# Opening a fused two-block transformer kernel in quarters of the features

## The chip, the cores and the metric

The kernel runs on 1 core of one Trainium2 chip. The metric is the device time of one execution in microseconds; lower is better. The kernel before took 1553.04 us (median of 3 runs, 1551.54 to 1555.72).

## The reference, cut to what matters

The program computes two transformer blocks over 256 tokens of 1024 features, all in float32: a first one (HGRN2 branch, windowed attention branch, 32-expert mixture) and a second one (stick-breaking attention, convolution, 32 smaller experts). The change is in the first few operations of the first block:

```python
cond = jax.nn.silu(c)                                   # (1, 1024)
mod = cond @ w_ada[l] + b_ada[l]                        # (1, 6144): sh1, sc1, g1, sh2, sc2, g2
h = rms_norm(x, norm1_gain[l]) * (1.0 + sc1) + sh1      # (256, 1024)
proj = h @ w_in[l]                                      # 1024 x 4864, in ten column blocks
hq, hf, hi, hg, aq, ak, av, gate_h, gate_a = split(proj)
```

Feature k of h needs only its own entries of sc1 and sh1, that is one column each of w_ada; but the sum over k in h @ w_in needs all 1024 features, in any order.

## The kernel before, in words

Every engine has its own instruction list, written out by hand in one order; semaphores join them. There is no planner.

Large weights arrive by DMAs of 2 MB that SyncE (SP) issues from one list, `PRE` (line 95), each into one of the numbered slots. An entry waits until the unit that was in its slot has been used (`unit_free`). All small things come otherwise: rows of c, lower bounds, convolution weights and gains, part of the constants, positions and b_ada by ten DMAs that ScalarE issues (lines 1175 to 1184), and nine gains, sinks and biases plus six pieces of router weights by DMAs that GpSimd issues (lines 1119 to 1133), the first nine counted by the semaphore `smalls`.

`ada(n)` (line 1514) multiplies one 2 MB unit of w_ada by the conditioning vector. Units ada 0 to 3 hold, for all of sc1 and sh1, two of the eight groups of 128 input features each; so no entry of the modulation is complete before all four units have been summed. Then VectorE adds b_ada (line 1984), TensorE transposes the row into columns (line 1542), and VectorE forms shift and scale columns (lines 1988, 1989).

`x` is normalised by VectorE (line 1958), transposed by TensorE (`transpose_h`), and modulated twice: ScalarE writes the upper part `hT_up` in the fast float32r type (line 1207), VectorE writes it in full (line 1996) and subtracts (line 2003), which gives `hT_low`.

The projection runs in rounds; round r is column block r of w_in. In each, a weight piece is split in the same way: `split_upper` (ScalarE, line 359) and `split_lower` (VectorE, line 364), 2048 columns each; the lower half of piece 0 alone is made by GpSimd (line 1114). TensorE then sums three products: upper by upper, lower by upper, upper by lower. Round 0 (aq, 512 columns, `first_tokens`) is two pieces of four feature groups each; round 1 (ak and av, 256 columns) is one piece; round 2 (hf) and round 3 (hq) are two pieces each, cut by columns, 96 products of 256 columns. TensorE's order is round 0, ada 4, round 1, round 2, ada 5, ada 6, round 3, then the transposes of q and k (line 1563).

After round 1 VectorE copies keys and values, waits for ScalarE's squares (`qk_squares`), sums them (line 2030), splits the next weight piece between two steps of the normalisation (line 2041), scales (2035 to 2038), splits another (2043) and rotates (2051 to 2056); this order stays as it is. `keep_warm_short(n, bank)` issues n products of the identity, whose result nobody reads.

Of the kernel before, what the change touches and what calls it, by code (L numbers as in the profile page):

```python
# [65 lines left out]
NFIRST = CONST["inv_freq"][0] + CONST["inv_freq"][1]  # L66

# [3 lines left out]
for _n, _w in [("w_r1", KD * NE), ("w_r2", KD * 36), ("hg_gain", 128), ("q_gain", 64), ("k_gain", 64), ("sink", 8),  # L71
               ("b_r1", NE), ("b_r2", 36), ("q_gain2", 64), ("k_gain2", 64), ("cols", 36), ("shiftT", 8), ("scaleT", 8), ("cond", 8), ("lb", 4),
               ("one_lb", 4), ("lbd", 4), ("posf", 2), ("ss", 4), ("rs", 2), ("ang", 16), ("rn", 16), ("rr", 16), ("cos", 16),
               ("sin", 16), ("decay", 16), ("ssh", 8), ("rsh", 8), ("ssa", 32), ("rsa", 32), ("m", 16), ("nm", 16),
               ("es", 16), ("den", 16), ("cond32", KD * 32)]:
    SMALL[_n] = (_at, _w)
    _at += _w
NSMALL = _at

# [5 lines left out]
             st=(24, 2), kt=(26, 10), kdT=(26, 4), o=(30, 4), qk=(36, 6), pT1=(36, 4), gates=(42, 16), s=(58, 12),  # L85
# [9 lines left out]
PRE_UNITS = [(("ada", 0, 0), 0), (("ada", 0, 1), 1), (("ada", 0, 2), 2), (("ada", 0, 3), 3), (("in", 0), 9), (("in", 1), 0),  # L95
# [16 lines left out]
def program(nc, t, out):  # L112
    ctx = ExitStack()
    with ctx:
# [21 lines left out]
        consts = sb("consts", [P, NCONST])  # L136
# [3 lines left out]
        ring1 = sb("ring1", [P, SLOTW])  # L140
        with nc.sbuf_tensor("below", [P, A1MAP["kt"][0] * KB], F32) as below, nc.sbuf_tensor("rows", [66, P], F32) as rows, \
                nc.sbuf_tensor("pos", [66, P], I32) as pos:
            pass
# [3 lines left out]
        def C(name):  # L147
            a, n = CONST[name]
            return consts[:, a:a + n]
# [5 lines left out]
        def at(m, name, lo=0, n=None, mem=arena):  # L155
# [4 lines left out]
        ident = C("ident")  # L160
        slots = [ring4[:, i, :] for i in range(4)] + [ring2[:, i, :] for i in range(2)] \
            + [at(M2MAP, n) for n in ("x0", "x1", "x2")] + [at(A1MAP, "gates")] + [ring1[:, :]]
# [30 lines left out]

        def slot_used(u):

            return SLOT_OF[u] in SLOT_OF[:u]
# [11 lines left out]
        def unit_load(eng, u, desc, done=None):  # L208
# [4 lines left out]
            if kind == "ada":  # L213
                _, b, kp = desc
                dst = slots[s].rearrange("p (k n) -> p k n", k=2)
# [13 lines left out]
        def loaded(u):  # L229

            return S(f"loaded{SLOT_OF[u]}"), 16 * SLOT_OF[:u + 1].count(SLOT_OF[u])
# [48 lines left out]
        BY_K, BY_COLS, WHOLE, BRANCH = range(4)  # L280

        def kind_of(r):
# [4 lines left out]
            if r < R2:  # L287
                return WHOLE if n == 1 else BY_COLS if n in (2, 3, 6, 7, 8, 9) else BY_K
            return BY_COLS if 3 <= n < 10 else BY_K

        def slot_r(s_):
            return ring4_r[:, s_, :] if s_ < 4 else at(A1MAP, "gates", mem=arena_r)

        PIECES = []
        for r_ in range(len(ROUNDS)):
            u_, _, half_, _ = ROUNDS[r_]
            both = (slots[SLOT_OF[u_]], slot_r(SLOT_OF[u_]))
            if kind_of(r_) == BRANCH:
                PIECES.append((r_, True) + tuple(a.rearrange("p (k n) -> p k n", k=4)[:, :, 512 * half_:512 * (half_ + 1)]
                                                 for a in both))  # L300
            elif kind_of(r_) == WHOLE:
                PIECES.append((r_, True) + tuple(a[:, 0:2048].rearrange("p (k n) -> p k n", k=KD) for a in both))
            else:
                for i_ in range(2):
                    if kind_of(r_) == BY_COLS:
                        PIECES.append((r_, i_ == 1) + tuple(a.rearrange("p (k n) -> p k n", k=KD)
                                                            [:, :, 256 * i_:256 * (i_ + 1)] for a in both))
                    else:
                        PIECES.append((r_, i_ == 1) + tuple(a[:, 2048 * i_:2048 * (i_ + 1)]
                                                            .rearrange("p (k n) -> p k n", n=512) for a in both))  # L310
# [4 lines left out]
        T_SEEN = dict(n2=2, n4=7)  # L315
        X_SEEN = dict(n2=0, n4=4)
        RMS_SEEN = dict(n2=1, n4=5)
# [15 lines left out]
        def upper(n):  # L333

            m = n % 3
            return ring2_r[:, m // 2, 2048 * (m % 2):2048 * (m % 2) + 2048]\
                .rearrange("p (k n) -> p k n", k=PIECES[n][2].shape[1])
# [14 lines left out]
        def split_upper(act, n):  # L352
            if n == 0:
                act.wait_ge(S("first_half"), 16)
# [6 lines left out]
        def split_lower(v, n):  # L361
            v.wait_ge(S("w_upper"), n + 1)
            _, _, w, w_r = PIECES[n]
            nc.vector.tensor_tensor(w_r, w, upper(n), ALU.subtract).then_inc(S("w_lower"), 1)  # L364

# [37 lines left out]
        FREE_UPPER = (len(PIECES) - 3) % 3  # L403
# [29 lines left out]
        def quad_loaded(q, i):  # L433
# [5 lines left out]
            return S(f"loaded{s_}"), 16 * ((s_ in HALVED) + SLOT_OF[:MOE2].count(s_) + fills)  # L439
# [71 lines left out]
        def h_cols(k):  # L511

            return PS[:, k // 4 * 2:k // 4 * 2 + 2, (k % 4) * P:(k % 4 + 1) * P]

# [5 lines left out]
        def rms_end(act, n, squares, first_half, second_half):  # L520
# [9 lines left out]
            def root(tile):  # L530
                act.wait_ge(S("mean_square"), RMS_SEEN[n] + 1 + tile)
# [8 lines left out]
            if squares is None:  # L540
                act.wait_ge(S("hT_A"), 2)
# [400 lines left out]
        def _(sp):  # L942
# [5 lines left out]

            sp.dma_start(x[:, :, :], t["x"][0].rearrange("(t p) d -> p t d", p=P)).then_inc(S("x"), 16)
            for u, d in enumerate(PRE):  # L950
                if slot_used(u):
                    wait(sp, unit_free(before_in_slot(u)))
                if u == IN0:
                    w = in_block(0, False)
                    for half, name in ((0, "first_half"), (1, f"loaded{SLOT_OF[u]}")):
                        sp.dma_start(slots[SLOT_OF[u]][:, 2048 * half:2048 * (half + 1)].rearrange("p (k n) -> p k n", n=512),
                                     w[:, 4 * half:4 * half + 4, :]).then_inc(S(name), 16)
                    sp.dma_start(consts[:, NFIRST:], t["consts"][:, NFIRST:]).then_inc(S("consts"), 16)
                else:
                    unit_load(sp, u, d)  # L960
                if d == ("in", 5):
# [144 lines left out]
        def _(pool):  # L1106
# [6 lines left out]
            pool.wait_ge(S("w_upper"), 1)  # L1113
            nc.gpsimd.tensor_tensor(PIECES[0][3], PIECES[0][2], upper(0), ALU.subtract).then_inc(S("first_lower"), 1)  # L1114
# [3 lines left out]
            wait(pool, loaded(IN0))  # L1118
            small_load(sm("hg_gain"), bc(t["hg_norm_gain"][0]), "smalls")
            small_load(sm("q_gain"), bc(t["q_norm_gain"][0]), "smalls")  # L1120
            small_load(sm("k_gain"), bc(t["k_norm_gain"][0]), "smalls")
            small_load(sm("q_gain2"), bc(t["q_norm_g_2"][0]), "smalls")
            small_load(sm("k_gain2"), bc(t["k_norm_g_2"][0]), "smalls")
            small_load(sm("sink"), bc(t["attn_sinks"][0]), "smalls")
            small_load(sm("b_r1"), bc(t["b_router"][0]), "smalls")
            small_load(sm("b_r2", 4), bc(t["b_router_group_2"][0]), "smalls")
            small_load(sm("b_r2")[:, 4:36], bc(t["b_router_expert_2"][0]), "smalls")
# [1507 lines left out]
```

## Time and profile before

| what | us |
|---|---|
| median of 3 runs | 1553.04 |
| the profiled execution, its own time | 1556.43 |
| its span, first to last instruction | 1554.6 |
| TensorE matmul busy | 1449.6 (93%) |
| VectorE busy | 602.7 (39%) |
| ScalarE busy | 342.5 (22%) |
| bytes moved | 594.74 MB, mean 383 GB/s |

All times inside the profile are counted from the first instruction. A line of the timeline is: start, duration, engine, line of the kernel, operation, output and input names, number of instructions merged; a bracket gives the idle time before and what ended it. PE is a product on TensorE and PEld the load of its stationary operand. A float32 product that isn't float32r shows as two instructions (six keep-warm products as x12). Durations of products overlap, so a rate is read from starts, or from a piece of the chain of waits.

### The profile page before, as it was taken

Reading aid. Unit: us, or ns where it says so; the run is one execution under the profiler, and the core shown is the slowest. Engines: PE = TensorE matmul, PEld = TensorE weight load, DVE = VectorE, ACT = ScalarE, POOL = GpSimd, SP = SyncE. Lnnn points to the kernel's source line nnn. Section 1 sums busy time; section 2 is a strip of 40 time slices with the busy share of each in tenths; the row PEclk is TensorE's granted clock in tenths of the full one; section 3 lists DMA queues with packets and bytes.
Section 4 is the critical chain, followed back from the end, with each engine's and each line's share of the span. In section 5 each row is a group of like instructions: output and inputs, shape, how many; then the busy total and the mean of one; then the engine's idle time right before and its main releaser. Section 6 shows DMA issues by size and latency. Waiting matters only on the chain.

```text
span 1554.6 us, 20816 instructions
## 1 busy us (share of the span) xinstructions
PE 1449.6 (93%) x8692; PEld 760.0 (49%) x8692; DVE 602.7 (39%) x920; ACT 342.5 (22%) x395; POOL 22.7 (1%) x36
## 2 busy tenths in 40 slices
PE   5999999999999999999998989999989999998677
PEld 2878985333333333333332333333338999854343
DVE  4686684232223232231321322322337687522111
ACT  4564332010001010110100100101023383421110
POOL 2100100000000000000000000000000000000000
PEclk9999999999999999999999989999999999999889
DMA  9986589999999999999999999999996446899997
GB/s 399 367 322 263 192 350 394 430 427 430 428 428 412 430 427 429 428 429 427 428 428 429 427 424 429 428 427 428 430 425 236 163 163 248 353 419 427 426 429 324
DMA packets 45575, 594.74 MB, mean 383 GB/s; under 512 B 5402, under 2 KB 5632, under 8 KB 9156
## 3 DMA queue, kind: packets, MB, share of 16 engines
q1 hardware_dynamic: 43184, 588.25, 90.5%
q0 software_dynamic: 1792, 4.86, 1.0%
q8 instruction: 55, 0.90, 0.2%
q10 hardware_dynamic: 532, 0.64, 0.1%
q14 instruction: 12, 0.10, 0.0%
HBM read 592.66 MB, written 1.06 MB: 382 GB/s over the span
## 4 chain that ended last, share of the span: by engine, by line
PE 58%; DMA 36%; DVE 3%; issue 1%; ACT 1%; POOL 0%; SPq 0%; DVEq 0%; ACTq 0%; POOLq 0%
PE PS L582 53%; DMA ring<-in_w_up 26%; DMA ring<-in_w_up_e 3%; DMA ring<-in_w_down_e 3%; DMA ring<-in_w_gate_e 2%; PE PS L762 2%; DMA arena<-in_w_in 2%; PE PS L782 1%; PE PS L1523 1%; DVE ring_r L364 1%; DMA arena<-mod_rows 1%; DVE arena L872 1%; PE PS L698 1%; ACT ring_r L359 0%; POOL arena_r L1114 0%
## 5 line engine op out<-in xcount | busy, mean ns | idle before, releaser
L582 PE MATMUL PS<-ring,arena 128*64 128x512 f32 x3020 | 672.4, 598 | 38.7 <-DMA ring<-in_w_up 25.6
L582 PEld LDWEIGHTS PS<-ring,arena 128*64 128x64 f32 x3020 | 212.7, 137 | 460.6 <-issue 403.7
L582 PE MATMUL PS<-arena 128*128 128x128 f32 (+12 forms) x1240 | 230.0, 443 | 2.9 <-DVE arena L2102 0.9
L860 DVE TENSOR_SCALAR arena<-PS 128x512 f32<-128x512 f32 x32 | 22.1, 691 | 481.0 <-PE PS L582 481.0
L561 ACT ACTIVATE arena<-arena 128x512 f32<-128x512 f32 x32 | 20.2, 630 | 697.4 <-DVE arena L860 697.4
L582 PE MATMUL PS<-ring_r 128*128 128x256 f32 (+1 forms) x576 | 171.5, 305 | 0.1
L582 PEld LDWEIGHTS PS<-arena 64*128 64x128 f32 (+6 forms) x1240 | 108.9, 165 | 121.4 <-issue 115.9
L582 PE MATMUL PS<-hT_r,ring_r 128*128 128x256 f32 x800 | 151.5, 286 | 0.3 <-DVE ring_r L364 0.3
L364 DVE TENSOR_TENSOR ring_r<-ring,ring_r 128x2048 fp32r<-128x2048 f32 x51 | 116.4, 2291 | 36.7 <-ACT ring_r L359 35.6
L582 PEld LDWEIGHTS PS<-hT_r,ring_r 128*128 128x128 f32 x800 | 127.6, 193 | 2.3 <-issue 1.4
L359 ACT ACTIVATE ring_r<-ring 128x2048 fp32r<-128x2048 f32 x51 | 97.2, 1912 | 103.9 <-PE PS L582 100.8
L582 PEld LDWEIGHTS PS<-ring_r 128*128 128x128 f32 x576 | 110.2, 192 | 5.2 <-DVE ring_r L2392 0.5
L582 PE MATMUL PS<-ring_r,hT_r 128*128 128x512 f32 (+1 forms) x336 | 99.2, 383 | 2.9 <-ACT hT_r L1207 1.4
L762 PE MATMUL PS<-ring,arena 128*32 128x256 f32 x704 | 50.9, 425 | 22.5 <-DMA ring<-in_w_up_e 9.8
L582 PEld LDWEIGHTS PS<-ring_r,hT_r 128*128 128x128 f32 x336 | 61.9, 188 | 18.1 <-issue 3.8
L854 DVE TENSOR_TENSOR x<-x,PS 128x2048 f32<-128x2048 f32 x31 | 70.6, 2278 | 0.0
L882 DVE TENSOR_TENSOR arena<-PS,arena 128x512 f32<-128x512 f32 x32 | 22.1, 691 | 118.8 <-PE PS L582 118.8
L762 PEld LDWEIGHTS PS<-ring,arena 128*32 128x32 f32 x704 | 29.7, 122 | 42.0 <-issue 31.8
L582 PE MATMUL PS<-arena_r,ring_r 128*128 128x256 f32 x352 | 45.2, 278 | 0.0
L872 DVE COPY arena<-PS 128x512 f32<-128x512 f32 x32 | 22.1, 691 | 56.9 <-PE PS L698 56.9
L582 PEld LDWEIGHTS PS<-arena_r,ring_r 128*128 128x128 f32 x352 | 43.2, 188 | 0.2 <-issue 0.2
L561 ACT ACT_TABLE_LOAD x31 | 39.8, 1283 | 1.1 <-issue 0.5
(384 smaller groups left out, 1004.5 us busy)
## 6 DMA issues: line engine op xcount, KB each, us to landing
ring<-in_w_up SPq DMA_DIRECT2D x128, 2048.0 KB, 20.9
ring<-in_w_down SPq DMA_DIRECT2D x59, 2048.0 KB, 18.8
ring<-in_w_in SPq DMA_DIRECT2D x17, 2048.0 KB, 10.8
ring<-in_w_ada SPq DMA_DIRECT2D x12, 2048.0 KB, 15.5
ring<-in_w_gate_e SPq DMA_DIRECT2D x11, 2048.0 KB, 35.5
ring<-in_w_down_e SPq DMA_DIRECT2D x10, 2048.0 KB, 27.0
ring<-in_w_up_e SPq DMA_DIRECT2D x10, 2048.0 KB, 29.8
arena<-in_w_gate_e SPq DMA_DIRECT2D x5, 2048.0 KB, 23.8
```

Source lines behind the costliest of these rows:

```text
L359: nc.scalar.activation(upper(n), PIECES[n][2], ACT.Copy).then_inc(S("w_upper"), 1)
L364: nc.vector.tensor_tensor(w_r, w, upper(n), ALU.subtract).then_inc(S("w_lower"), 1)
L561: nc.scalar.activation(sg, glu, ACT.Sigmoid, scale=1.702).then_inc(S(f"{X}_sg"), 1)
L582: return nc.tensor.matmul(o, w, m, start=first, stop=last)
L698: mm_ = nc.tensor.transpose(PS[:, 1, i * P:(i + 1) * P], actb[:, i * P:(i + 1) * P], ident)
L762: mm_ = nc.tensor.matmul(PS[q, 2 + i, 0:256], xg2[:, k * P + CAP2 * j:k * P + CAP2 * (j + 1)], moe2_weights(where, 2 * i + j // 2, j % 2, ...
L782: mm_ = nc.tensor.matmul(PS[q, b, :], aT2[:, kk * P + CAP2 * j:kk * P + CAP2 * (j + 1)], down_weights(where, j, kk, b), start=kk == 0, sto ...
L854: V.tensor_tensor(xflat, xflat, PS[:, 4:8, :].rearrange("p b n -> p (b n)"), ALU.add).then_inc(S(f"{X}_added"), 1)
L860: V.tensor_scalar(glu.rearrange("p (kk b q) -> p kk b q", kk=4, b=2), hu[:, :, :, :, 0], 7.0, None, ALU.min)\
L872: V.tensor_copy(aT, PS[:, 1, :]).then_inc(S(f"{X}_aT"), 1)
L882: V.tensor_tensor(ye[:, 0:512], PS[:, 1, :], g2h, ALU.mult).then_inc(S(f"{X}_ye"), 1)
L1523: last = nc.tensor.matmul(PS[32 * j:32 * j + 32, 7, :], sm("cond32")[:, 32 * k:32 * k + 32], w[:, kk, 512 * j:512 * (j + 1)], start=k == 0 ...
```

## The change

- The columns of sc1 and sh1 are laid out again in quarters: unit q (2 MB) now holds everything for features 256q to 256q+255, all 1024 input features. The first 1 MB of unit 0 has a semaphore of its own.
- w_in's blocks 0, 1 and 2 are transferred in quarters of the features too (`opening_part`), in the order x, unit 0, block 0 quarter 0, unit 1, blocks 1 and 2 quarter 0, block 0 quarter 1, unit 2, and so on.
- TensorE's opening: 20 keep-warm products, unit 0, transposes by a product with a diagonal of the inverse roots (so x isn't scaled first), `mod_columns`, 6 keep-warm products; then for each quarter a quarter of round 0, the next quarter's unit, a quarter of round 1, half a quarter of round 2, the next quarter's `mod_columns`, the other half. ada 4 follows all that, then round 3 (`split_cols(3)`), ada 5 and ada 6.
- `mod_columns` replaces the transposes of the modulation row: four products with a moving operand of one column. The transposed, normalised x goes through an SBUF copy (`hN`), made by ScalarE.
- The pieces of rounds 0 to 2 are 12 instead of 5, of 1024, 512 and 1024 columns; all lower halves are VectorE's. Round 3's first piece is now number 12, split inside the normalisation of q and k, where pieces 5 (round 3) and 4 (round 2) stood in and ahead of it before.
- Small inputs are packed on the host: `first` (52 columns and the constants that the opening needs, 752 bytes per partition) is ScalarE's first DMA; `packed` (router weights, gains, sinks, biases; 1004 columns) is one DMA of SP behind the opening's weights, instead of 15 of GpSimd.
- Slots of the units of `PRE` change: block 5 goes to slot 0, which block 3 leaves at the end of round 3 (before: slot 2, left at the end of round 2). The early load of 2 MB for expert 7 is issued after block 7 instead of block 5.
- Later lines change only in counts and indices.

```diff
-PRE_UNITS = [(("ada", 0, 0), 0), (("ada", 0, 1), 1), (("ada", 0, 2), 2), (("ada", 0, 3), 3), (("in", 0), 9), (("in", 1), 0),
-             (("ada", 1, 0), 1), (("in", 2), 2), (("ada", 1, 1), 3), (("in", 3), 9), (("ada", 1, 2), 1), (("in", 4), 0),
-             (("ada", 1, 3), 3), (("in", 5), 2), (("ada", 2, 0), 1), (("in", 6), 3), (("ada", 2, 1), 0), (("in", 7), 1),
+PRE_UNITS = [(("ada", 0, 0), 0), (("ada", 0, 1), 3), (("in", 0), 9), (("in", 1), 11), (("in", 2), 10), (("ada", 0, 2), 2),
+             (("ada", 0, 3), 1), (("in", 3), 0), (("ada", 1, 0), 3), (("ada", 1, 1), 2), (("in", 4), 1), (("ada", 1, 2), 3),
+             (("ada", 1, 3), 9), (("in", 5), 0), (("ada", 2, 0), 2), (("in", 6), 3), (("ada", 2, 1), 9), (("in", 7), 1),
...
SyncE:
+            mod_load(0)
+            for q in range(PARTS):
+                for r in range(OPENING):
+                    sp.dma_start(opening_part(r, q)[0], in_block(r, False)[:, 2 * q:2 * q + 2, :])\
+                        .then_inc(opening_landed(r, q)[0], 16)
+                    if r == 0 and q < PARTS - 1:
+                        mod_load(q + 1)
+            sp.dma_start(small[:, 0:NPACKED], t["packed"][:, :]).then_inc(S("smalls"), 16)
+            sp.dma_start(consts[:, NCOLS + NFIRST:], t["consts"][:, NFIRST:]).then_inc(S("consts"), 16)
...
ScalarE:
+            act.dma_start(consts[:, 0:NCOLS + NFIRST], t["first"][:, :]).then_inc(S("first"), 16)
+            act.dma_start(pos[:, :], t["positions"][:, :]).then_inc(S("rows"), 16)
+            act.wait_ge(S("first"), 16)
...
+            normed(0)
+            normed(1)
+            split_upper(act, 0)
+            normed(2)
+            upper_part(0)
+            normed(3)
+            split_upper(act, 1)
+            split_upper(act, 2)
+            for q in range(1, PARTS):
+                split_upper(act, OPENING * q)
+                upper_part(q)
+                split_upper(act, OPENING * q + 1)
+                split_upper(act, OPENING * q + 2)
...
TensorE:
+            pe.wait_ge(S("first"), 16)
+            keep_warm_short(20, 6)
+            pe.wait_ge(S("mod_in"), 1)
+            mod_products(0, 0)
+            pe.wait_ge(S("h"), TT)
+            transposed(0)
+            transposed(1)
+            mod_products(0, 1)
+            transposed(2)
+            transposed(3)
+            pe.wait_ge(S("mod_in"), 2)
+            mod_columns(0)
+            keep_warm_short(6, 6)
+            for q in range(PARTS):
+                opening_tokens(0, q)
+                if q == 0:
+                    pe.wait_ge(S("hN"), PARTS)
+                if q < PARTS - 1:
+                    mod_products(q + 1, 0)
+                    mod_products(q + 1, 1)
+                opening_tokens(1, q)
+                opening_cols(2, q, lambda: mod_columns(q + 1) if q < PARTS - 1 else None)
             ada(4)
-            pe.wait_ge(S("hT_V"), 1)
-            split_tokens(1)
-            keep_warm_short(6, 4)
-            split_cols(2)
+            split_cols(3)
             ada(5)
             ada(6)
-            split_cols(3)
...
VectorE:
+            def modulated(q):
+                v.wait_ge(S("ada_done"), q + 1)
+                sig(CP(mod_sums[:, q % 2, :], PS[:, 7, :]), "modrow")
+                v.wait_ge(S("rowsT"), q + 1)
+                a, ks = 4 * q, slice(2 * q, 2 * q + 2)
+                L(TV(sm("mod_cols")[:, a:a + 4], PS[:, 4, a:a + 4], cols[:, 36 + a:40 + a], ALU.add))
+                sig(TV(sm("scaleT")[:, ks], sm("mod_cols")[:, a + 2:a + 4], cols[:, 28 + 2 * q:30 + 2 * q], ALU.mult), "modT")
+                v.wait_ge(S("hN"), q + 1)
+                for kk in range(2):
+                    k = 2 * q + kk
+                    last = TS(h_full[:, k, :], hN[:, k, :], sm("scaleT")[:, k:k + 1], sm("mod_cols")[:, a + kk:a + kk + 1],
+                              ALU.mult, ALU.add)
+                L(last)
+                v.wait_ge(S("hT_A"), 2 * q + 2)
+                sig(TV(hT_low[:, ks, :], h_full[:, ks, :], hT_up[:, ks, :], ALU.subtract), "hT_lower")
+            for q in range(PARTS):
+                modulated(q)
+                for r in range(OPENING):
+                    split_lower(v, OPENING * q + r)
...
-            L(head_norm(qk, 12, at(A1MAP, "qkT"), [(0, 8, "q_gain"), (8, 4, "k_gain")], 1, lambda: split_lower(v, 5),
+            L(head_norm(qk, 12, at(A1MAP, "qkT"), [(0, 8, "q_gain"), (8, 4, "k_gain")], 1, lambda: split_lower(v, 12),
                         True))
-            split_lower(v, 6)
+            split_lower(v, 13)
```

## Rows read from the trace of the kernel before

**Rows 1.** The page, the chain that ended last, by engine.

```profile
PE 58%; DMA 36%; DVE 3%; issue 1%; ACT 1%; POOL 0%; SPq 0%; DVEq 0%; ACTq 0%; POOLq 0%
```

**Rows 2.** The chain in order of time: start us, us, what; 0 to 260 us.

```profile
3.43 25.07 DMA arena<-in_w_in
...
37.29 7.61 PE PS L582 x32
...
46.75 18.79 PE PS L582 x156
...
69.11 11.52 PE PS L582 x96
```

**Rows 3.** The same chain, in the first mixture of experts.

```profile
798.21 25.51 DMA ring<-in_w_up
```

**Rows 4.** Windows: us, PE, PEld, DVE, ACT, POOL busy (instructions), clock, DMA share, GB/s.

```profile
0.00:32.30 32.30, 14.17 (x98) 5.99 (x98) 10.83 (x40) 10.53 (x18) 1.98 (x5) 1.00 0.94 392
...
65.50:80.50 15.00, 15.00 (x130) 12.37 (x130) 14.72 (x24) 12.65 (x13) 1.50 (x2) 1.00 0.87 333
80.50:114.30 33.80, 32.52 (x191) 22.78 (x189) 30.26 (x33) 21.86 (x42) 2.66 (x4) 1.00 0.79 311
```

**Rows 5.** DMA issues: KB each and median us from issue to landing.

```profile
ring<-in_w_in SPq DMA_DIRECT2D x17, 2048.0 KB, 10.8
...
ring<-in_w_hg_branch SPq DMA_DIRECT2D x1, 2048.0 KB, 7.8
...
x<-in_x SPq DMA_DIRECT2D x1, 1024.0 KB, 4.9
...
out<-x SPq DMA_DIRECT2D x2, 256.0 KB, 2.4
...
consts<-in_consts ACTq DMA_DIRECT2D x1, 68.0 KB, 10.7
```

**Rows 6.** Timeline of TensorE's products, 0 to 75 us.

```profile
15.25 6.03 PE L1523 MATMUL PS<-ring,small 128*32 128x512 f32 x32 [1.60 <-DVE small L1947]
...
26.05 1.92 PE L1523 MATMUL PS<-ring,small 128*32 128x512 f32 x16 [0.88 <-DMA ring<-in_w_ada]
...
29.38 1.50 PE L582 MATMUL PS<-consts 128*128 128x128 f32 x12
```

**Rows 7.** Timeline of TensorE's weight loads, 12 to 40 us.

```profile
19.52 0.20 PEld L1523 LDWEIGHTS PS<-ring,small 128*32 128x32 f32 x4 [0.66 <-issue]
...
23.71 0.13 PEld L1523 LDWEIGHTS PS<-ring,small 128*32 128x32 f32 x4 [0.30 <-issue]
```

**Rows 8.** Timeline of VectorE, 0 to 75 us.

```profile
52.73 0.88 DVE L2015 COPY arena<-PS 128x128 f32<-128x128 f32 x4 [0.76 <-PE PS L582]
...
53.97 2.29 DVE L364 TENSOR_TENSOR ring_r<-ring,ring_r 128x2048 fp32r<-128x2048 f32 x1
60.11 1.75 DVE L2030 TENSOR_REDUCE small<-arena 128x24 f32<-128x1536 f32 x1 [3.85 <-DMA small<-in_b_router_expert]
...
62.11 2.29 DVE L364 TENSOR_TENSOR arena_r<-arena,ring_r 128x2048 fp32r<-128x2048 f32 x1
...
68.44 2.29 DVE L364 TENSOR_TENSOR arena_r<-arena,ring_r 128x2048 fp32r<-128x2048 f32 x1
```

**Rows 9.** VectorE's waits, 66 to 115 us: us in all, times, longest.

```profile
DVE arena L2102 <- PE PS L582: 1.4, 2, 0.7
```

**Rows 10.** Timeline of ScalarE, 0 to 135 us.

```profile
15.63 1.04 ACT L1192 ACTIVATE hT<-x 128x1024 f32<-128x1024 f32 x1
...
54.03 1.49 ACT L1234 ACTIVATE arena<-arena 128x1536 f32<-128x1536 f32 x1 [2.58 <-DVE arena L2016]
...
82.99 1.93 ACT L359 ACTIVATE ring_r<-ring 128x2048 fp32r<-128x2048 f32 x1
...
86.23 0.85 ACT L1260 ACTIVATE arena<-arena 128x768 f32<-128x768 f32 x1 [0.80 <-DVE arena L2079]
88.22 1.06 ACT L1260 ACTIVATE arena<-arena 128x1024 f32<-128x1024 f32 x1 [1.14 <-DVE arena L2079]
```

More of the change, by code:

```diff
@@ L192, in program, with landings @@
         SLOT_OF = [slot_of(u) for u in range(MOE2 + NSLOT)]
+        def landings(s, before):
+            return SLOT_OF[:before].count(s)
         def slot_used(u):
@@ L275, in wait @@
             eng.wait_ge(sv[0], sv[1])
[L280 removed]
+        BY_K, BY_COLS, BRANCH = range(3)
         def kind_of(r):
@@ new lines, in program, with halves_of @@
+        OPENING, PARTS = 3, 4
+        def halves_of(r):
+            d = ROUNDS[r][1]
+            cn = 512 if d[0] == "out" else (IN_COLS if r < R2 else IN_COLS2)[d[1]][1]
+            both = (slots[SLOT_OF[ROUNDS[r][0]]], slot_r(SLOT_OF[ROUNDS[r][0]]))
+            if kind_of(r) == BY_COLS:
+                return [[a.rearrange("p (k n) -> p k n", k=KD)[:, :, 256 * i:256 * (i + 1)] for a in both] for i in range(2)]
+            return [[a[:, 4 * cn * i:4 * cn * (i + 1)].rearrange("p (k n) -> p k n", n=cn) for a in both] for i in range(2)]
@@ L1537, in _, with mod_products @@
-            ada(2)
-            ada(3)
-            pe.wait_ge(S("modrow"), 1)
-            for c in range(4):
-                last = nc.tensor.transpose(PS[:, 4, c * P:(c + 1) * P], modrow[:, 0, c * P:(c + 1) * P], ident)
-            last.then_inc(S("rowsT"), 1)
-            keep_warm_short(6, 7)
-            first_tokens()
+            def mod_products(q, c):
+                wait(pe, (S("mod_first"), 16) if q == 0 and c == 0 else loaded(ADA[q]))
+                for k in range(4 * c, 4 * c + 4):
+                    j = k % 4
+                    last = nc.tensor.matmul(PS[32 * j:32 * j + 32, 7, :], sm("cond32")[:, 32 * k:32 * k + 32],
+                                            slots[SLOT_OF[ADA[q]]][:, 512 * k:512 * (k + 1)],
+                                            start=c == 0, stop=c == 1, tile_position=(0, 32 * j))
+                if c == 1:
+                    last.then_inc(S("ada_done"), 1)
@@ new lines, in opening_cols @@
+            def opening_cols(r, q, between=None):
+                n, o = q * OPENING + r, PS[:, banks(r), :].rearrange("p b (c t) -> p (b c) t", c=2)
+                ks = slice(2 * q, 2 * q + 2)
+                wu, wl, xu, xl = upper(n), PIECES[n][3], hT_up[:, ks, :], hT_low[:, ks, :]
+                wait(pe, lower_ready(n))
+                for c in range(4):
+                    cs = slice(c * P, (c + 1) * P)
+                    for k in range(2):
+                        for m, (a, w) in enumerate(((xu, wl), (xl, wu), (xu, wu))):
+                            last = mm(o[:, c, :], w[:, k, cs], a[:, k, :],
+                                      q == 0 and c % 2 == 0 and k == 0 and m == 0,
+                                      q == PARTS - 1 and c % 2 == 1 and k == 1 and m == 2)
+                    if between and c == 1:
+                        between()
+                last.then_inc(S("big_done" if q == PARTS - 1 else "half_done"), 1)
@@ L2626 @@
     arrays, t = {}, {}
-    for name in _INS + ["consts", "last_down"]:
-        a = CONSTS if name == "consts" else last_down(inputs["w_down_e_2"]) if name == "last_down" else laid_out(name, inputs[name])
+    made = dict(consts=CONSTS, first=np.concatenate([columns(inputs), CONSTS[:, 0:NFIRST]], 1), packed=packed(inputs), w_ada_first=first_modulation(inputs["w_ada"]),
+                b_ada_rows=inputs["b_ada"].reshape(3, 4, 512)[1:3].transpose(1, 0, 2), last_down=last_down(inputs["w_down_e_2"]))
+    for name in _INS + list(made):
+        a = np.ascontiguousarray(made[name]) if name in made else laid_out(name, inputs[name])
         arrays[f"in_{name}"] = a
```

433 lines of the change are left out of this document (204 added, 229 removed).

## The prediction

> **What bounds the kernel now.** I read the page's chain of waits by engine first: TensorE 58%, DMA 36% [rows 1]. Then the chain in order of time. In the mixture of experts it steps from DMA to DMA, 25.5 us of waiting for weights per expert with short pieces of TensorE [rows 3]; these transfers go into slots that the work before frees, so a microsecond saved ahead of them moves them all. At the start the chain is one wait of 25.07 us for block 0 of w_in, behind x and the four modulation units [rows 2], at 392 GB/s and 0.94 of the DMA engines' time [rows 4]. From 37.29 us on it is TensorE without gaps: rounds 0 to 2 up to 65.5, adas 5 and 6, round 3 from 69.11 to 80.63 [rows 2]. VectorE hardly rests either: 14.72 of 15.00 us between 65.5 and 80.5, 30.26 of 33.80 until 114.3 [rows 4]. So the change has two clocks to move: TensorE's end of round 3 and ada 6 (80.63), and VectorE's normalisation of q and k, which begins at 60.11 after 3.85 us of waiting for the small inputs [rows 8]. What comes out of 80.63 should reach the end.
>
> **The change part by part.** Times are on the span's clock; T is when the first real product of round 0 starts.
>
> *Start.* TensorE's first wait is for `first`, 96 KB. Bounds from landings: 2.4 us after issue (256 KB at the end of the kernel) to 10.7 us (68 KB of constants, fifth in ScalarE's queue, beside 2 MB transfers) [rows 5]; issued at 0.75, that is 3.2 to 11.5. It is nearest to x, the same instant on the other queue, 4.9 us for 1 MB [rows 5], and ten times smaller; I take 4.9 on the clock. Then 20 keep-warm products, 40 instructions. Warm, one takes about 0.118 (12 in 1.50 with the last one's tail) [rows 6]. TensorE begins slow: its weight loads with the idle time before them take 0.86 us at 19.52 and 0.43 at 23.71 [rows 7], half rate against full (1.2 against 2.4 GHz), though the column says 1.00. TensorE had started at 15.25 [rows 6], so about 4.7 us go slow. That is 20 instructions, and the other 20 take 2.3: 7.0 us, until 11.9. Beside it ScalarE and VectorE make h's diagonal: squares 2 x 1.04 [rows 10], the rest DMA issue, table load and small operations that I estimate at 4.6 us after `first`, together 11.6. That is hidden by only 0.3; were it later, T moves by as much.
>
> Then half a unit (1.92 for 16 instructions [rows 6], so 0.93), eight products with the diagonal (16 x 0.118 = 1.9), the other half (0.93), eight more (1.9), `mod_columns`, six keep-warms (1.4). No row shows a product with one moving column. Eight instructions cost between 0.3 (estimated from a third of a keep-warm's) and 1.0 (a keep-warm's full 0.12 each); I take 0.7. T = 4.9 + 7.0 + 5.7 + 0.7 + 1.4 = 19.7. The weights for it are there: 3.5 MB (3.67 million bytes) at 392 GB/s [rows 4] behind 0.75 and a small landing's 2.4 [rows 5] make 12.5. The last keep-warms hide VectorE's columns and ScalarE's first upper part.
>
> *A quarter.* Round 0: 12 products, 32 took 7.61 [rows 2], so 2.86. A unit: 1.85. Rounds 1 and 2: 12 and 24 products of 256 columns; 156 instructions took 18.79 [rows 2], 0.120 each, so 1.44 and 2.9. `mod_columns` 0.7. Sum 9.75. The transfers for a quarter are 3.25 MB, 8.7 us at 392 GB/s, and started earlier: hidden. The chain from `mod_columns` to the next quarter (VectorE adds and multiplies, ScalarE writes one upper group, about 1.0) lies beside the other half of round 2's quarter, 1.45; the cover is 0.4 to 0.5, and VectorE's 5 us of work per quarter fits into 9.75. If the cover goes, each quarter waits (rival C).
>
> Round 1 ends at R = T + 3 x 9.75 + 2.86 + 1.44 = 53.2; the opening ends at 56.1.
>
> *VectorE after round 1.* Before: copies from 52.73, a weight split of 2.29 (53.97), 3.85 of waiting, reduce at 60.11 [rows 8]. Now the split and the wait for small inputs are gone (`packed` lands near 40). Late next is ScalarE's square, 1.49 [rows 10], behind the copies, 1.24: reduce at R + 2.85 = 56.1, 4.0 earlier. The order behind it is kept.
>
> *TensorE after the opening.* ada 4, until 58.0. Round 3 needs the lower half of piece 12, which VectorE makes inside the normalisation: before it ended at 62.11 + 2.29 = 64.4, 4.3 after the reduce began [rows 8], without anyone waiting. Now it comes at R + 7.15 = 60.4: a new wait of 2.4. Half of the round is 48 x 0.120 = 5.8, until 66.1; the second piece is ready 10.6 after the reduce (68.44 + 2.29) [rows 8], at R + 13.5 = 66.7: 0.6 more. Round 3 ends at 72.5, adas 5 and 6 (69.11 - 65.54 = 3.6 [rows 2]) at 76.1. Before: 80.63. TensorE gains 4.5, VectorE 4.0. VectorE had 1.4 us in hand at 99 to 101, where it waited for TensorE's scores [rows 9], so 4.0 hardly holds back 4.5. I take 4.4.
>
> *The queues.* SP's opening list is longer by some dozen issues of 0.4 us, all early. 0.5 MB of small things ride in it, 1.3 us of transfer behind the last weights of the opening: hidden. GpSimd's 15 loads and its split vanish; they bound nothing but the 3.85 above. The early load for expert 7 goes behind block 7; between 80.5 and 114.3 DMA is busy 0.79 [rows 4] and its reader comes far later: nothing. Block 5 is now issued at the end of round 3, 72.5. By the nearest landing of 2 MB on a quiet queue, 7.8 [rows 5], it arrives at 80.3; ScalarE wants it at 82.99 - 4.4 = 78.6 and had 0.80 and 1.14 in hand at 86.23 and 88.22 [rows 10], 1.9 against a delay of 1.7: hidden, barely (rival E otherwise).
>
> Sum: -4.4 us. The profiled execution took 1556.43, so it would take 1552.0; it lies 3.4 above the median 1553.04, from which I get 1548.6. What this kernel's measurement can tell from no change is about 0.3%, 4.7 us; the forecast lies just inside.
>
> **The rivals.**
> A, the forecast: round 3 waits for VectorE, 1548.6; own range 1546.8 to 1550.5, which is T plus or minus 1.9.
> B, the start is shorter: `first` at 3.2 (-1.7) and the columns at 0.3 (4 x 0.4 = -1.6). The gain is 7.7: 1545.3. For it: 96 KB is little. Against: h's diagonal then ends no sooner than x's landing allows.
> C, slower than before: the hand-off between quarters is exposed. Place: `mod_columns(q + 1)`, which stands in the middle of round 2's quarter; VectorE must have copied the sums (0.7) by then. It decides once VectorE comes more than 1.0 late there, for instance behind its three splits and the rotary angles, which it does first. Then TensorE stands before `mod_columns` and again before the next quarter. Taking copy 0.7, small operations 0.5, upper parts 1.0, and the full-precision part and its subtraction 1.4 as uncovered, 3.6 of it three times is 10.8, of which VectorE's gain of 4.0 and TensorE's of 4.5 don't survive: 4.4 - 10.8 = -6.4, 1559.4. Against: VectorE's 5 us fit into 9.75.
> D, `first` lands late. The constants' 10.7 us for 68 KB [rows 5] speak for it: T = 26.3, gain 4.4 - 6.6 = -2.2, 1555.2. Half way (8.2) gives 1551.9. Against: only x and half a unit stand on the other queue when it starts.
> E, block 5 comes late. With the median landing of 10.8 [rows 5] it is there at 83.3, 4.7 after it is wanted; less the 1.9 in hand 2.8 are lost: gain 1.6, 1551.4. It stands for any later place where the shift is eaten, too.
>
> The Trainium skill says under DMA: Bandwidth & Descriptors (Queues, rings and completion order) that each DMA engine takes turns between queues, a whole packet of many descriptors at a time. By that rule ScalarE's small transfer pays a whole packet of SP's at each turn, as in D; the constants' slow landing agrees with it, and the rule would give a time between D's two.
>
> **How the numbers follow.** A 0.50, B 0.24, C 0.07, D 0.07, E 0.12. Faster by over 0.3% (below 1548.4): 0.21 of A, all of B: 0.45. Slower (above 1557.7): C's 0.06. Same: 0.49. The range 1544.0 to 1554.0 holds A, E, half of D and most of B; C, the rest of D and the lower end of B are outside.
>
> **What would show it.** In the changed profile: `first` releasing TensorE near 5 us; keep-warms until about 12; the first float32r product near 19.7; quarters 9.7 us apart; no wait for DMA after the first quarter. Round 1 ends near 53, the reduce starts near 56 behind ScalarE's square and not behind a DMA. A gap of 2 to 3 us on TensorE ahead of round 3, put down to VectorE's split. The transposes of q and k near 76 instead of 80.63, and the same distance up to the first expert. It is wrong if round 3 starts with no gap (then more is won), if quarters are 12 us apart (C), or if the gain at 76 is not there at 240.

## The result and the profile after

The changed kernel takes 1556.07 us (median of 20 runs, 1552.62 to 1560.01) against 1554.03 for the kernel before on the same chip (20 runs, 1550.62 to 1556.35): ratio 1.0016, 95% interval 1.0009 to 1.0024, that is 2.5 us slower (1.4 to 3.7). The forecast was 4.4 us faster. (The ratios here are not the quotients of the medians; that would be 1.0013.) Its profiled execution took 1554.78 us, less than the 1556.43 of the one before; the order of two single executions says nothing, as the last section shows.

The page of the changed kernel, its TensorE row and the chain by engine, the one that answers to [rows 1]:

```profile
span 1553.0 us, 21046 instructions
...
PE 1459.1 (94%) x8762; PEld 768.4 (49%) x8762; DVE 605.9 (39%) x940; ACT 346.6 (22%) x407; POOL 8.8 (1%) x20
...
PE 56%; DMA 38%; DVE 4%; issue 1%; ACT 1%; SPq 0%; DVEq 0%; ACTq 0%; POOLq 0%
```

TensorE is busy 9.5 us longer and the whole is no shorter. The chain in order of time (start, duration, what) shows the opening, against [rows 2]:

```profile
0.75 4.42 DMA consts<-in_first
...
5.22 7.09 PE PS L614 x40
12.31 1.00 PE PS L1535 x8
13.31 1.98 PE PS L614 x16
15.29 0.99 PE PS L1535 x8
16.29 2.78 PE PS L614 x24
...
30.75 0.59 ACT hT_r L1220
...
31.44 0.70 DVE ring_r L2041
...
32.17 1.24 DVE arena_r L395
...
33.45 1.20 PE PS L614 x4
34.65 1.85 PE PS L1535 x16
36.50 3.82 PE PS L614 x32
```

The long wait for block 0 is gone; `first` lands 4.4 us after its issue. From then on the chain goes through every quarter of round 0 in the same way: ScalarE writes an upper part, VectorE subtracts (L2041), splits the weights (L395), and TensorE takes its three groups of four products, each when its part is ready. The timeline has the same quarter:

```profile
31.04 1.12 PE L614 MATMUL PS<-ring_r,hT_r 128*128 128x512 f32 x4
32.19 1.20 PE L614 MATMUL PS<-ring_r 128*128 128x512 f32 x4
33.45 1.20 PE L614 MATMUL PS<-arena_r,hT_r 128*128 128x512 f32 x4
34.58 0.64 PE L1535 MATMUL PS<-ring,small 128*32 128x512 f32 x4
```

The groups start 1.15, 1.26 and 1.13 us apart; four of the 32 products of [rows 2] make 0.95. No bracket shows idle time, since the durations of products reach over it; the starts show it. The quarters stand 10.63 to 10.67 us apart (20.37, 31.04, 41.67, 52.30).

VectorE behind round 1 (timeline, in brackets the idle time before and what ended it), against [rows 8]:

```profile
57.37 0.88 DVE L2082 COPY arena<-PS 128x128 f32<-128x128 f32 x4 [0.99 <-PE PS L614]
...
60.30 1.75 DVE L2096 TENSOR_REDUCE small<-arena 128x24 f32<-128x1536 f32 x1 [1.71 <-ACT arena L1256]
...
62.30 2.29 DVE L395 TENSOR_TENSOR ring_r<-ring,ring_r 128x2048 fp32r<-128x2048 f32 x1
```

The wait for small inputs is gone, as forecast, and the sum starts 2.95 us after round 1's end. But that end is at 57.35, so the sum starts at 60.30 where it was 60.11. TensorE around the start of round 3:

```profile
64.73 0.47 PE L614 MATMUL PS<-hT_r,ring_r 128*128 128x256 f32 x1 [2.72 <-DVE ring_r L395]
65.00 0.42 PE L614 MATMUL PS<-ring_r 128*128 128x256 f32 x1
65.21 0.63 PE L614 MATMUL PS<-hT_r,ring_r 128*128 128x256 f32 x2
...
68.20 0.30 PE L614 MATMUL PS<-ring_r 128*128 128x256 f32 x1
68.34 0.40 PE L614 MATMUL PS<-hT_r,ring_r 128*128 128x256 f32 x2
68.58 0.28 PE L614 MATMUL PS<-ring_r 128*128 128x256 f32 x1
...
81.48 1.53 PE L1628 MATMUL PS<-consts,arena 128*128 128x128 f32 x12
```

Behind a gap of 2.72 us the products start 0.215 us apart and from 68.2 on 0.120. The granted clock of that stretch (windows: stretch, length, PE busy, clock, DMA share, GB/s) falls with it; between 66 and 68.2 us it is 0.50, the lower of its two levels:

```profile
60.00:65.00 5.00, 2.28 (x20) 0.98 0.49 141
65.00:70.00 5.00, 5.00 (x31) 0.68 1.01 431
70.00:75.00 5.00, 5.00 (x44) 1.00 0.73 311
```

Sixteen products took 3.47 us, where 0.120 each makes 1.92: 1.5 us lost. The transposes of q and k (L1628) begin at 81.48. Those of p, the attention's probabilities and the next place that every version shares, begin at 129.19. In the kernel before it is 80.46 and 128.08:

```profile
80.46 1.47 PE L1563 MATMUL PS<-consts,arena 128*128 128x128 f32 x12
...
128.08 3.04 PE L1600 MATMUL PS<-consts,arena 128*128 128x128 f32 x24
```

### The profile page after: what moved, and what is told of

Its sections match the earlier page's. It is cut to its first block, busy times and chain, and to the rows that moved or that the text cites. A ratio compares the mean times of both kernels' runs of the same rounds, so it can differ in the third digit from the quotient of the medians.

```text
span 1553.0 us, 21046 instructions
## 1 busy us (share of the span) xinstructions
PE 1459.1 (94%) x8762; PEld 768.4 (49%) x8762; DVE 605.9 (39%) x940; ACT 346.6 (22%) x407; POOL 8.8 (1%) x20
## 4 chain that ended last, share of the span: by engine, by line
PE 56%; DMA 38%; DVE 4%; issue 1%; ACT 1%; SPq 0%; DVEq 0%; ACTq 0%; POOLq 0%
PE PS L614 50%; DMA ring<-in_w_up 29%; DMA arena<-in_w_gate_e 3%; DMA arena<-in_last_down 3%; DMA arena<-in_w_up_e 2%; PE PS L794 2%; DVE ring_r L395 1%; PE PS L814 1%; PE PS L1525 1%; DMA arena<-mod_rows 1%; DVE arena L904 1%; PE PS L730 1%; PE PS L1535 0%; DVE arena_r L395 0%; DMA consts<-in_first 0%
## 5 line engine op out<-in xcount | busy, mean ns | idle before, releaser
L614 PE MATMUL PS<-hT_r,ring_r 128*128 128x256 f32 x832 | 157.6, 289 | 3.1 <-DVE ring_r L395 3.1
L614 PEld LDWEIGHTS PS<-hT_r,ring_r 128*128 128x128 f32 x832 | 133.8, 196 | 5.9 <-issue 5.0
L395 DVE TENSOR_TENSOR ring_r<-ring,ring_r 128x2048 fp32r<-128x2048 f32 (+1 forms) x54 | 119.1, 2212 | 30.7 <-ACT ring_r L390 29.6
L390 ACT ACTIVATE ring_r<-ring 128x2048 fp32r<-128x2048 f32 (+1 forms) x54 | 99.5, 1846 | 103.3 <-PE PS L614 101.2
L614 PEld LDWEIGHTS PS<-ring_r,hT_r 128*128 128x128 f32 x320 | 58.6, 188 | 18.1 <-issue 2.7
## 6 DMA issues: line engine op xcount, KB each, us to landing
ring<-in_w_down SPq DMA_DIRECT2D x59, 2048.0 KB, 19.7
```

What stands on the lines that cost most here:

```text
L390: nc.scalar.activation(upper(n), PIECES[n][2], ACT.Copy).then_inc(S("w_upper"), 1)
L614: return nc.tensor.matmul(o, w, m, start=first, stop=last)
```

## The experiments

Every version was timed against the kernel before on the same chip; a ratio of 1.0010 is 1.6 us. The kernel before had medians of 1553.44 us beside the first four, 1553.86 beside the second, 1553.15 beside the third and 1553.76 beside the last three. The last column gives the starts of q and k's transposes and of p's in the one profiled execution of each.

| version | median us (runs) | ratio to before, 95% | q,k / p at us |
|---|---|---|---|
| e1_after (changed kernel, again) | 1555.71 (12) | 1.0013, 1.0002 to 1.0023 | 81.2 / 128.9 |
| e1_gap | 1555.96 (12) | 1.0018, 1.0009 to 1.0027 | 80.7 / 128.4 |
| e1_delay | 1561.82 (6) | 1.0054, 1.0037 to 1.0070 | 86.5 / 134.1 |
| e1_early | 1554.38 (12) | 1.0005, 0.9994 to 1.0017 | 80.6 / 128.2 |
| e2_order | 1553.89 (12) | 1.0004, 0.9994 to 1.0015 | 76.8 / 127.2 |
| e2_inter | 1556.65 (10) | 1.0019, 1.0010 to 1.0028 | 80.1 / 127.8 |
| e2_both | 1552.36 (11) | 0.9995, 0.9985 to 1.0004 | 76.0 / 125.4 |
| b_packed | 1553.62 (11) | 1.0001, 0.9989 to 1.0013 | 80.5 / 128.1 |
| e3_bshift | 1555.07 (11) | 1.0014, 1.0005 to 1.0023 | 80.7 / 128.3 |
| e3_ashift | 1555.84 (11) | 1.0015, 1.0003 to 1.0028 | 79.7 / 127.4 |
| e3_both (e2_both again) | 1552.55 (11) | 1.0001, 0.9991 to 1.0011 | 75.8 / 126.1 |
| e3_bothshift | 1552.98 (12) | 0.9997, 0.9987 to 1.0007 | 76.6 / 126.1 |
| e4_after | 1552.93 (12) | 1.0008, 0.9995 to 1.0021 | 81.2 / 128.9 |
| e4_both | 1552.69 (12) | 0.9990, 0.9977 to 1.0003 | 76.0 / 125.4 |
| e4_b64 | 1554.51 (12) | 1.0009, 1.0000 to 1.0019 | 80.6 / 128.2 |

**First four: is the shift eaten later, and what does the clock cost?** The changed kernel again:

> The changed kernel as it is, as the yardstick for the others of this call. Every theory: about 1.0013 of the kernel before (+2.0 us), round 3 released by VectorE's split some 2.7 us after ada 4, and products at half rate for some 3 us behind that wait.

e1_gap fills the wait ahead of round 3:

```diff
             ada(4)
+            keep_warm_short(12, 4)
             split_cols(3)
```

> The changed kernel with 12 keep-warm products (24 instructions, 2.8 us) between ada 4 and round 3, so that TensorE is never idle there; no real product starts earlier. Clock theory (the half-rate stretch after the 2.7 us wait costs 1.5 us, and TensorE's place at 80 us reaches the end): the products of round 3 stand 0.12 us apart from the first on, the transposes of q and k come near 80.1 instead of 81.55, and the time is 1 to 1.5 us below the changed kernel's. Rival (VectorE's chain or the experts' transfers set the end): the products are faster but the time stays within 0.5 us of the changed kernel's.

The clock stayed up: its windows are

```profile
60.00:65.00 5.00, 5.00 (x45) 1.00 0.46 128
65.00:70.00 5.00, 5.00 (x43) 1.00 1.00 424
```

but the transposes came only 0.5 to 0.8 us sooner, to 80.7 and not the 80.1 expected, for the split came 0.2 later and the second one then held TensorE for 0.3. The gain of 1 to 1.5 us did not come (1.0018 after 1.0013), though intervals of 1.4 us to either side could hide the 0.5 to 0.8. So the lost clock explains a part of the lateness at 81 us and is no lever by itself.

e1_delay starts the kernel before later, e1_early issues its early load behind block 7:

```diff
-            keep_warm_short(6, 7)
+            keep_warm_short(46, 7)
             first_tokens()
...
-                if d == ("in", 5):
+                if d == ("in", 7):
```

> The kernel before with 46 keep-warm products instead of 6 ahead of round 0: everything behind it, on TensorE and VectorE, comes 9.4 us later. Pass-through theory (a microsecond at 80 us is a microsecond at the end): 9 to 9.5 us slower than before. Rival (the experts' transfers have a lead of their own and swallow part of it): at 240 us the profile is 9.4 behind, at the end of the experts clearly less; 3 to 6 us slower.

> The kernel before with one edit, the 2 MB early load for expert 7 issued after block 7 instead of after block 5, as the changed kernel has it. If this transfer order costs what the changed kernel lost: 1 to 2 us slower than before. If it is hidden, as predicted: within 0.5 us of before.

The 40 more keep-warms were to cost 9.4 us and cost 6.0 at the transposes of q and k: the rest went into waits that round 0 of the kernel before has anyway,

```profile
32.31 2.10 PE L582 MATMUL PS<-ring_r,hT_r 128*128 128x512 f32 x8 [1.43 <-ACT hT_r L1207]
35.13 2.13 PE L582 MATMUL PS<-arena_r,hT_r 128*128 128x512 f32 x8 [0.72 <-POOL arena_r L1114]
```

and into the slower starts behind them. From there the 6.0 stand undiminished at p's transposes, and the time is 8.4 us longer (5.7 to 10.9). A shift that reaches 128 us reaches the end, as far as a width of 5 us tells; its single profile ends only 1.2 us after the other, 1555.8 for 1554.6. The early load costs nothing that can be told, but its interval (0.9 faster to 2.6 slower) holds both the 0.5 and most of the 1 to 2 us that it was to decide between; its place at p is 0.1 us from the kernel before.

**Second four: which of the waits matter?** e2_order puts piece 12's split ahead of the normalisation on both engines; e2_inter puts the next quarter's modulation products where TensorE waits inside round 0:

```diff
             sig(CP(vv, o[:, :, 128:256]), "big_free_V")
+            split_lower(v, 12)
...
-            L(head_norm(..., lambda: split_lower(v, 12), True))
-            split_lower(v, 13)
+            L(head_norm(..., lambda: split_lower(v, 13), True))
```

```diff
                 for m, (a, w) in enumerate(((xu, wu), (xl, wu), (xu, wl))):
+                    if m and between:
+                        mod_products(between[0], m - 1)
```

> The changed kernel with piece 12 split ahead of the squares (ScalarE's upper half before the squares, VectorE's lower half before the sum), and piece 13 in its place inside the normalisation. Path theory (TensorE's wait of 2.7 us and the half-rate stretch behind it are what round 3 costs): no wait of TensorE ahead of round 3, the transposes of q and k near 77.4 instead of 81.5, VectorE's sum about 1 us later but its rotation about 1.4 us earlier; 2 to 4 us faster than the changed kernel, so 1 to 2 us faster than before. Rival (the loss sits elsewhere): no change.

> The changed kernel with the next quarter's modulation products put between the three parts of round 0's quarter instead of behind them. Path theory (TensorE waits for VectorE twice in each quarter of round 0, 0.7 us in all): three quarters are 10.0 instead of 10.6 us long, round 1 ends near 55.3 instead of 57.3, and everything behind it on both engines comes 2 us earlier; 2 us faster than the changed kernel, level with before. Rival (the quarter's length is the products' own): no change.

> Both edits. Path theory: round 1 ends near 55.3, the transposes come near 75.3, VectorE is 3.5 us ahead of the changed kernel; about 5 us faster than it and 3 faster than before. Rivals: as for the single edits.

The chain of e2_inter has no VectorE in its first three quarters any more, but a group of round 0, half a unit, and so on:

```profile
19.97 1.15 PE PS L614 x5
21.12 0.99 PE PS L1535 x8
22.11 1.12 PE PS L614 x4
23.24 0.99 PE PS L1535 x8
24.23 5.79 PE PS L614 x44
```

Its quarters are 10.35 to 10.39 us apart, not 9.75. By the starts, a group of four still takes 1.05 to 1.14 where another kind of product (float32, 32 columns of weights) stands behind it, and half a unit 1.00 instead of 0.93: 0.07 to 0.19 goes at each such change. The waits of 0.2 and 0.3 were traded for two more changes, and 0.27 of the 0.88 came back. The 2 us expected of this edit did not come: 1.0019, as slow as the changed kernel. e2_order brings q and k's transposes 4.7 us forward, to 76.8, close to the 76.1 of the forecast; but p's only 2.0. It was to be 1 to 2 us faster than before and is 0.6 slower (0.9 faster to 2.3 slower). One reason is that TensorE now waits for VectorE. Its waits from 82 to 126 us (us in all, times, longest) have a new first line:

```profile
PE PS L614 <- DVE arena L2163: 1.7, 1, 1.7
PE PS L614 <- DVE arena L2168: 0.9, 1, 0.9
```

where the kernel before has 0.9 and 0.3. The other is the clock behind that wait, 0.79 from 96 to 104 us. In e2_both, with the same wait, it stays at 1.00 and p's transposes begin at 125.4; in the same kernel run again, e3_both, it is 0.79 and they begin at 126.1. With both edits p's transposes are 2.7 us earlier than before. By e1_delay that should have been 2.7 us at the end. It was 0.8 (from 2.3 faster to 0.6 slower): something in the kernels made from the changed one costs time behind 128 us.

b_packed gives the kernel before only the one packed load:

```diff
+                    sp.dma_start(small[:, 0:NPACKED], t["packed"][:, :]).then_inc(S("smalls"), 16)
...
-            v.wait_ge(S("smalls"), NSMALLS)
+            v.wait_ge(S("smalls"), 16)
```

> The kernel before with one part of the change alone: small inputs and router weights come packed, in one transfer of SyncE behind the constants, instead of 15 of GpSimd. VectorE's wait of 3.85 us ahead of its sum goes. If TensorE sets the pace there: at most 1.3 us faster than before (its own waits for VectorE at 99 and 114). If VectorE does: 3 to 4 us faster. If the 0.5 MB in the opening's queue hurts: slower, with round 1 or 2 waiting for their weights.

```profile
56.17 1.75 DVE L2015 TENSOR_REDUCE small<-arena 128x24 f32<-128x1536 f32 x1
```

VectorE's sum moves from 60.11 to 56.17, and the transposes of q and k and of p stay where they were. VectorE's 3.85 us of waiting were worth nothing that can be told while TensorE set the pace: the 3 to 4 us of the other theory lie outside the interval (1.7 faster to 2.0 slower).

**Third four: where an array lies.** Between the transposes of ho, the HGRN2 branch's output, and the next norm lies the same code in all versions, and their profiles fall into two classes: 43.0 to 43.3 us in the four made from before, 43.9 to 44.1 in the six made from the changed kernel. It is one group of products, here in the kernel before and in the changed one (start, duration):

```profile
187.02 22.01 PE L582 MATMUL PS<-arena_r,ring_r 128*128 128x256 f32 x192
```

```profile
189.46 23.03 PE L614 MATMUL PS<-arena_r,ring_r 128*128 128x256 f32 x192
```

What differs for them is the place of the arena in SBUF. `consts` grew by 52 columns and `small` shrank by 28, so every array behind them, ring1 and the arena, lies 96 bytes higher: the arena at 149280 instead of 149184.

```diff
-NSMALL = _at
+NSMALL = _at + 24
```

This is e3_bshift; e3_ashift and e3_bothshift have 8 in place of 24.

> The kernel before with 24 unused columns behind `small`: ring1 and the arena begin 96 bytes higher in each partition, 149280 instead of 149184, as in the changed kernel; so the arena is no longer on a multiple of 64 bytes. Nothing else differs. In every profile so far the 192 products of the branches (out<-in PS<-arena_r,ring_r, 128x256) take 22.01 us in the kernels built from before and 23.03 in those built from the changed one, and from the transposes of ho to the next norm it is 43.0 to 43.3 against 43.9 to 44.1. Layout theory: here the 192 products take 23.0, that stretch 43.9 to 44.1, and the whole is 1 to 2 us slower than before (ratio 1.0006 to 1.0013). Rival, order theory (the slots, the list of transfers or the pieces' numbers make it): 22.0, 43.0 to 43.3, ratio 1.0000.

> The changed kernel with 8 unused columns behind `small`: ring1 and the arena begin 32 bytes higher, at 149312, which is again a multiple of 64 bytes as in the kernel before (149184). Layout theory with a grain of 64 bytes: the 192 branch products take 22.0 instead of 23.03, the stretch from the transposes of ho to the next norm 43.0 to 43.3, and the whole is 1 to 2 us faster than the changed kernel's 1.0013 to 1.0018: ratio 1.0003 to 1.0010. Order theory: 23.0, 44.0, ratio 1.0013 to 1.0018.

> The same kernel as the one with the splits of pieces 12 and 13 put forward and the next quarter's modulation products put between the parts of round 0, run again beside the one that follows, so that they share a chip. Both theories: 0.9995 again, 0.9985 to 1.0004; the q and k transposes at 76, those of p at 125.

> The same with the 8 unused columns, arena at 149312. Layout theory: 1 to 2 us faster than without them, ratio 0.9982 to 0.9990, the first to beat the kernel before clearly. Order theory: equal to the run without them, 0.9995.

The kernel before with nothing but the 96 bytes:

```profile
187.26 23.03 PE L582 MATMUL PS<-arena_r,ring_r 128*128 128x256 f32 x192
```

and it is 1.0014 (1.0005 to 1.0023) times as slow. The place costs slightly more than expected (1.0006 to 1.0013), and the order theory falls. My rule of 64 bytes fell with it: at 149312 the group takes 22.86, and the time does not improve, neither in e3_ashift (1.0015, where 1.0003 to 1.0010 was expected) nor in e3_bothshift (0.9997 beside 1.0001 for e3_both, where 0.9982 to 0.9990 was).

**Last three: the address of before, exactly.** In e4_after and e4_both `rn` and `rr` share the room of `den` and `es`, so the arena is back at 149184; e4_b64 moves the arena of before to 149248:

```diff
-... ("ang", 16), ("rn", 16), ("rr", 16), ("cos", 16)
+... ("ang", 16), ("unused", 8), ("cos", 16)
+SMALL["rn"], SMALL["rr"] = SMALL["den"], SMALL["es"]
```

> The changed kernel with its arena back at exactly 149184, the address in the kernel before (two scratch entries of `small` share the room of two others, which are used later, and 8 unused columns keep the distance). Layout theory: the 192 branch products take 22.0 us instead of 23.03, 43.0 to 43.3 from the transposes of ho to the next norm, and the ratio falls from 1.0013 to 1.0018 to 1.0003 to 1.0008, which is the opening's own loss of about 1 us. Rival: something else of the change costs the time; 22.0 us all the same, but a ratio of 1.0013 or more.

> The version with the splits put forward and the modulation products between the parts of round 0, its arena at 149184. Layout theory: p's transposes at 125.5 to 126, 2.3 earlier than before, the 192 products in 22.0, and a ratio of 0.9982 to 0.9988, faster than before with certainty. Rival: 0.9995 to 1.0000, as the version measured without the move.

> The kernel before with 16 unused columns behind `small`, the arena 64 bytes higher, at 149248. The multiple of 64 at 149312 gave 22.86 in place of 22.01 to the changed kernel. If the exact place within 128 or 256 bytes matters, the 192 products take between 22.2 and 23.0 here and the ratio is 1.0004 to 1.0012; if a distance of 64 bytes is harmless, 22.0 and 1.0000.

The changed kernel at the old address, then the kernel before 64 bytes off, in the groups of products (instructions, busy us and mean ns of one, idle before):

```profile
L615 PE MATMUL PS<-arena_r,ring_r 128*128 128x256 f32 x352 | 45.2, 278 | 0.0
```

```profile
L582 PE MATMUL PS<-arena_r,ring_r 128*128 128x256 f32 x352 | 46.4, 283 | 0.0
```

In the timeline the 192 of them take 22.01 and 23.03. The second is just above the 22.2 to 23.0 expected for e4_b64, so the exact place matters even at a distance of 64 bytes. e4_after's ratio of 1.0008 is the upper end of the 1.0003 to 1.0008 that the layout theory asked for, but its interval reaches from 0.9995 to 1.0021 and takes in the rival's 1.0013, and the quotient of its medians is 0.9995: the products' rate is settled, the share of the whole only made likely. e4_both has the lowest ratio of all versions, 0.9990, short of the 0.9982 to 0.9988 expected; its interval (0.9977 to 1.0003) still holds no change.

## Why the prediction was wrong, step by step

The forecast and the result are 6.9 us apart. The opening came 5.4 us later than forecast, 3.4 of it in the quarters, whose cover by other work the prediction held to be sufficient; 1.0 us by the trace comes from an array whose place was not in the sum at all. The rest, about 0.5, is less than the measurement can tell.

**What bounds the kernel.** Right: TensorE sets the pace from 37 us on (b_packed), and a shift there reaches the end (e1_delay).

**Start.** Nearly right, 20.4 for 19.7: landing 4.4 us after issue against 4.15, keep-warms 7.09 against 7.0, and 0.3 more in the small steps behind them. h's diagonal was ready at 12.6, a microsecond later than forecast, and moved nothing: the text had it hidden by only 0.3, but half a unit stands in front of the first product that needs it. Neither B nor D: `first` landed near where the nearest row put it. The prediction took from the Trainium skill, DMA: Bandwidth & Descriptors (Queues, rings and completion order), the rule that engines take turns between queues by whole packets, and put the landing by it between 8.2 and 11.5 us on the clock, D's two; 94 KB beside x in 4.4 us give no sign of such a delay.

**A quarter.** This is where the step failed, and the largest error: 10.63 for 9.75, three times, 2.7 us, and 0.7 more in the last quarter (round 1 ended 5.05 us after its start, not 4.30). The prediction had followed the hand-off only to the upper part, which the first group needs; that cover held, for the first group starts without a gap. For the rest it had set VectorE's 5 us of work against 9.75 and called the cover sufficient. A sum of work says nothing of its order: inside the quarter TensorE's second group needs L2041 and its third L395, one behind the other, and nothing stood between to cover them. It is C's kind of wait, but at 0.5 per quarter instead of 3.6, and not at `mod_columns` but two steps on. The rest of the 0.88 is 0.18 for the change from round 0 to the unit, 0.08 for that from the unit to round 1 and 0.11 for `mod_columns` (0.81 from its start to the next product's, for 0.7); short groups have ends that a mean over 32 products in a row does not hold.

**VectorE after round 1.** The step was right to 0.1 us (2.95 for 2.85), its base was late: the 4.0 us that the packed inputs were to bring went to pay for the later end of round 1.

**TensorE after the opening.** The wait of 2.4 was there, 2.72. Not in the sum: the clock lost behind it, 1.5 us; in return the 0.6 at the second piece fell away. Round 3 lasted 13.2 us instead of 12.1. That loss is not certain to come: in e3_ashift, behind the same wait of 2.73, the clock stays at 1.00 and the round lasts 12.2, as forecast, while e1_after, e2_inter and e4_after lose it as the changed kernel does.

The forecast had the transposes at 76.1 and they came at 81.48, 5.4 later: 0.7 start, 2.7 quarters, 0.7 last quarter, 0.2 split, 1.1 round 3. That alone turns 4.4 us faster into 1.0 slower.

**The queues.** Block 5 was issued at 78.01, as much later as round 3 ended, and landed 8.0 us after that (forecast 7.8); ScalarE waited 1.99 for it, and TensorE's waits from 82 to 126 us are those of the kernel before, 0.9 and 0.3, so E is out. What was missing from this part: that a change in the size of a small array moves a large one. The text costed nothing for `consts` and `small`. That is 1.0 us in the branch products by the trace; on the whole 2.2 us (0.8 to 3.6) in e3_bshift and 1.4 (0.0 to 3.0) in e4_b64.

Together 1.0 and 1.0 make 2.0 slower, against 2.5 (1.4 to 3.7) and 2.0 (0.3 to 3.6) measured. What stays open: e2_inter, e1_gap and e3_ashift measured 3.0, 2.8 and 2.3 us slower where the same sum (the lateness of p's transposes and the place of the arena) gives 0.7, 1.3 and 0.2; the intervals are 1.6 to 4.4, 1.4 to 4.2 and 0.5 to 4.3. For e3_ashift 1.5 of the 2.1 are its one profiled execution, whose p stands at 127.4 where e1_after's is at 128.9, 0.9 of it because the clock stayed up. But all sixteen versions, the changed kernel included, measured above this sum, by 0.2 to 2.4 us and by 1.0 on average. So about 1 us, and up to 2 in single versions, may lie in something that the profiles do not show. And which places in SBUF are good: of four, 149184 gives 22.01, 149248 and 149280 23.03, 149312 22.86.

## What to carry to other kernels

Where work is cut finer, do not compare each engine's sum per piece with the time from one piece to the next: write out the chain inside a piece, what the second and third group need and who makes it, and see what stands between. When the last wait of one engine goes, ask first whether that engine sets the pace; 3.85 us vanished here and gave nothing that could be told. And when versions differ by a part in a thousand, compare a stretch of unchanged code in both traces: if its products run at another rate, see whether an array has moved, and pad the small arrays in front to keep it where it was.

## What the runs showed of the hardware

Products from the arena and the ring (128x256, float32r) run at 0.1146 us each with the arena at 149184 and at 0.120 with it at 149248 or 149280, the same program otherwise; the other products of 128x256 float32r, those of hT_r and ring_r, start 0.120 us apart (median) at every place tried.

TensorE came back from 2.72 us of idle time at close to half rate, 0.215 us for a product of 0.120, for 3.5 us; with the gap filled the clock stayed at 1.00. That happened in four of the five profiles with this wait; in e3_ashift the clock stayed at 1.00 without anything in the gap. A product with a moving operand of one column costs nearly as much as one of 128: from start to start an instruction takes 0.10 us against 0.12 for a keep-warm's.

Single executions differ by dips of the clock in the same code: in the window 133 to 155 us it was 0.92 in the execution before and 0.84 after.

```profile
133.00:155.00 22.00, 21.56 (x270) 0.92 0.52 204
```

```profile
133.00:155.00 22.00, 22.00 (x265) 0.84 0.51 217
```

From p's transposes to the next ones that took 24.9 and 26.2 us, in other executions 23.5. This dip cost the changed kernel more. What put the two profiled executions in the wrong order came later: the clock of the execution before was 0.52 from 460 to 474 us, 0.53 from 900 to 911 and 0.57 from 1344 to 1348, that of the changed kernel 0.65, 1.00 and 1.00. So a single profile tells places in the opening, and not the whole to 1 or 2 us.
